# Norm copies ahead of squares, blocks split early, two products behind the batches

## The reference

```
# block 1
x = x + diff_attention(rms_norm(x, g), w_qkv, ...)       # 1024 -> 3072 columns, 8 double heads
x = x + conv_ffn(rms_norm(x, g), ...)                    # 1024 -> 5632 -> 1024
x = x + mla_attention(rms_norm(x, g), ...)               # rank 384 queries, rank 256 keys and values
x = x + conv_ffn(rms_norm(x, g), ...)
x = rms_norm(x, final_norm_g)
# block 2
b, c, h = split(rms_norm(x, g) @ w_in, 3)                # short convolution mixer
x = x + (b * conv3(c * h)) @ w_out
x = x + peer(rms_norm(x, g), ...)                        # 16384 experts, 8 heads x top 16
x = x + windowed_gqa(rms_norm(x, g), ...)
x = x + peer(rms_norm(x, g), ...)
out = rms_norm(x, final_norm_g_2)
```

## Time and profile before

| | |
|---|---|
| runs | 2628.58, 2632.16, 2633.97 us (median 2632.16) |
| profiled execution | 2633.33 us, span 2631.4 us |
| TensorE busy | 2527.1 us, 96% |
| VectorE busy | 1971.2 us, 75% |
| ScalarE busy | 1288.7 us, 49% |
| GpSimd busy | 749.9 us, 28% |
| mean granted TensorE clock | 0.987 |
| DMA | 424.66 MB, mean 161 GB/s |

### The profile page before, as it was taken

One profiled execution on the slowest core, in us unless ns is written; L12 is line 12 of the kernel. 1 busy time (PEld: TensorE's weight loads), 2 busy tenths in 40 slices (PEclk: granted clock), 3 DMA queues, 4 the chain that ended last, 5 costly groups with the idle time before them and its releaser, 6 DMA issues.

```text
span 2631.4 us, 44294 instructions
## 1 busy us (share of the span) xinstructions
PE 2527.1 (96%) x14328; PEld 2219.6 (84%) x14328; DVE 1971.2 (75%) x3589; ACT 1288.7 (49%) x1917; POOL 749.9 (28%) x754
## 2 busy tenths in 40 slices
PE   7889997999999999999999999899999999999998
PEld 6779976898889898888888888779898888888887
DVE  6868767787567998567777777688998577777776
ACT  4756556665544165544444444573165444444443
POOL 0400004000000101255555555230101255555554
PEclk9989999999999999999999999999999999999999
DMA  5145641556554523666666665434424666666664
GB/s 194 59 130 182 199 144 48 153 183 200 169 167 149 154 67 112 208 185 190 190 191 191 190 191 185 144 98 159 137 65 136 208 186 190 191 190 191 191 190 145
DMA packets 169937, 424.66 MB, mean 161 GB/s; under 512 B 13374, under 2 KB 65982, under 8 KB 169071
## 3 DMA queue, kind: packets, MB, share of 16 engines
q1 hardware_dynamic: 166832, 418.86, 51.5%
q10 hardware_dynamic: 3006, 4.49, 0.5%
HBM read 420.11 MB, written 3.18 MB: 161 GB/s over the span
## 4 chain that ended last, share of the span: by engine, by line
PE 88%; DVE 6%; ACT 3%; issue 2%; POOL 1%; DMA 0%; DVEq 0%; SPq 0%; POOLq 0%; ACTq 0%
PE PS L467 18%; PE PS L468 18%; PE PS L469 18%; PE PS L731 13%; PE PS L820 8%; PE PS L733 7%; PE PS L846 4%; DVE lo L1524 1%; PE PS L788 1%; ACT arena L1087 1%; PE PS L640 0%; DVE arena L1943 0%; DVE arena L1732 0%; DVE xx L1572 0%; ACT arena L1028 0%
## 5 line engine op out<-in xcount | busy, mean ns | idle before, releaser
L1524 DVE TENSOR_TENSOR lo<-raw,hi 128x1024 fp32r<-128x1024 f32 x716 | 1060.1, 1506 | 494.4 <-ACT hi L988 493.3
L988 ACT ACTIVATE hi<-raw 128x1024 fp32r<-128x1024 f32 x716 | 747.6, 1053 | 306.3 <-PE PS L469 287.9
L467 PE MATMUL PS<-hi,Ah 128*128 128x512 f32 x1024 | 402.6, 393 | 11.5 <-issue 5.4
L468 PE MATMUL PS<-lo,Ah 128*128 128x512 f32 x1024 | 402.1, 393 | 0.0
L469 PE MATMUL PS<-hi,Al 128*128 128x512 f32 x1024 | 399.6, 390 | 0.0
L731 PE MATMUL PS<-xx,hi 128*128 128x512 f32 x1504 | 371.4, 389 | 0.0
L731 PEld LDWEIGHTS PS<-xx,hi 128*128 128x128 f32 x1504 | 282.3, 188 | 58.6
L467 PE MATMUL PS<-xx,hi 128*128 128x256 f32 x1152 | 329.2, 286 | 1.4 <-DVE xx L1572 1.4
L468 PE MATMUL PS<-xx,hi 128*128 128x256 f32 x1152 | 328.2, 285 | 0.0
L469 PE MATMUL PS<-xx,lo 128*128 128x256 f32 x1152 | 327.9, 285 | 0.0
L1429 ACT ACTIVATE gl<-gl 128x256 f32<-128x256 f32 x188 | 78.6, 418 | 483.6 <-DVE gl L2276 483.6
(11 more groups left out here) (247 smaller groups left out, 3577.9 us busy)
## 6 DMA issues: line engine op xcount, KB each, us to landing
raw<-in_peer_u SPq DMA_DIRECT2D x256, 512.0 KB, 3.6
raw<-in_peer_v SPq DMA_DIRECT2D x256, 512.0 KB, 4.4
raw<-in_ffn_w_up SPq DMA_DIRECT2D x88, 512.0 KB, 3.6
raw<-in_ffn_w_down SPq DMA_DIRECT2D x44, 512.0 KB, 4.2
raw<-in_peer_w_q SPq DMA_DIRECT2D x32, 512.0 KB, 4.5
raw<-in_da_w_qkv SPq DMA_DIRECT2D x24, 512.0 KB, 4.4
raw<-in_conv_w_in SPq DMA_DIRECT2D x24, 512.0 KB, 3.8
raw<-in_attn_w_qkv SPq DMA_DIRECT2D x12, 512.0 KB, 4.3
```

Source lines behind the costliest of these rows:

```text
L467: pe.matmul(o, ah, bh, start=start, stop=False)
L468: pe.matmul(o, ah, bl, start=False, stop=False)
L988: cp.activation(hi[:, s, 0:size], raw[:, s, 0:size], ACT.Copy).then_inc(hi_made, 1)
L1524: V.tensor_tensor(lo[:, s, 0:size], raw[:, s, 0:size], hi[:, s, 0:size].bitcast(F32), ALU.subtract).then_inc(lo_made, 1)
```

## The change

It does four things. At the start, the gains of the first norm are loaded by themselves, the high and low copies come ahead of the squares with block 0 and 1 split among them, the other parameters are loaded by SP behind the first four blocks, and the parameter arithmetic moves to behind `lo` 7. `mla_ukv`'s blocks are split two behind group 1 of `mla_uq` and all four ahead of its loop. `cout`'s first four blocks are split beside the last group of `cin`, and TensorE does half `h` = 0 of them first, waiting only for the first half of `actL`. The leads are spread wider, and the last two stand behind batch 63; ScalarE does their GELUs behind the splits of `v` blocks 0 and 1.

```diff
@@ -100,7 +100,7 @@
 LEAD_FIRST = 20
-LEAD_AFTER = (-1, 3, 8, 13, 18, 23, 28, 33, 38, 43, 48, 53, 58, 63)
+LEAD_AFTER = (-1, 3, 8, 14, 19, 24, 30, 35, 40, 46, 51, 57, 63, 63)
 KEPT = LEAD - 2
@@ -260,8 +260,8 @@
-        lamv = view(1024, 4, DA_DH)
-        lamp = view(1024 + 256, 2, DA_DH)
+        lamv = view(29700, 4, DA_DH)
+        lamp = view(29700 + 256, 2, DA_DH)
         hotv = view(29000, 512)
@@ -532,23 +532,24 @@
-                early = RING if name in ("down0", "down1") else 0
+                early = RING if name in ("down0", "down1", "cout") else 0
+                first = 0 if name == "cout" else 1
                 if not early:
                     acc_ready(G0)
-                acc_ready(G0 + 1)
+                acc_ready(G0 + first)
                 for kc in range(early):
...
                     for t in range(TT):
-                        part(kc, t, 1)
+                        part(kc, t, first)
                 if early:
-                    acc_ready(G0)
+                    acc_ready(G0 + 1 - first)
                 for kc in range(kcs - 2):
...
                     for t in range(TT):
-                        for h in range(1 if kc < early else 2):
+                        for h in (1 - first,) if kc < early else (0, 1):
                             i = part(kc, t, h)
@@ -950,8 +951,8 @@
                 acc_free[G0 + g] = [(S("mix_read"), g + 1)]
-            pe.wait_ge(S("mix_lo"), 2)
-            wide("cout", actH, actL, KD)
+            pe.wait_ge(S("mix_lo"), 1)
+            wide("cout", actH, actL, KD, {4: lambda: pe.wait_ge(S("mix_lo"), 2)})
             for layer in range(2):
@@ -1164,19 +1165,32 @@
-            def load(dst, src):
-                act.dma_start(dst, src).then_inc(params_in, 16)
-            load(con[:, P:], consts[:, P:])
-            load(lamv, laid_rows[:, 0:4 * DA_DH].rearrange("o (k d) -> o k d", d=DA_DH).to_broadcast([P, 4, DA_DH]))
...
-            act.wait_ge(S("columns_in"), 16)
-            norm("n0", G_ATTN)
+            def first_squares(t):
+                for q in (2 * t, 2 * t + 1):
+                    w = quarters[q][1]
+                    cp.activation(XS[:, t, w], X[:, t, w], ACT.Square, scale=D ** -0.5,
+                                  accum_out=ss[:, q:q + 1]).then_inc(sq_made, 1)
+            def first_root(t):
+                act.wait_ge(ms_made, t + 1)
+                cp.activation(ss[:, 6 + t:7 + t], ss[:, 4 + t:5 + t], ACT.Sqrt).then_inc(rt_made, 1)
+            act.wait_ge(S("set_up"), 1)
+            cp.activation(small[:, 58:59], ss[:, 4:5], ACT.Sqrt)
+            act.wait_ge(S("first_gain_in"), 16)
+            turned("n0", G_ATTN, 0, range(4))
             splits_to(1)
+            turned("n0", G_ATTN, 0, range(4, KD))
+            splits_to(2)
+            act.wait_ge(S("x_in0"), 16)
+            first_squares(0)
+            splits_to(3)
+            act.wait_ge(S("x_in1"), 16)
+            first_squares(1)
+            first_root(0)
+            first_root(1)
             act.wait_ge(S("rstd_made"), 1)
@@ -1198,6 +1212,7 @@
                     qkv_copy(g, it)
+            act.wait_ge(S("columns_in"), 16)
             act.wait_ge(S("rel_table"), 1)
@@ -1324,13 +1339,11 @@
                         lambda t, g: arena[:, 1344 + t * 1536 + g * 512:1344 + t * 1536 + (g + 1) * 512],
-                        {0: lambda: turned("mck", G_MKV, MLA_QR // P)})
+                        {0: lambda: turned("mck", G_MKV, MLA_QR // P), 1: lambda: splits_to(plan["mla_ukv"][0] + 2)})
             B, G0 = plan["mla_ukv"]
-            splits_to(B + 1)
+            splits_to(B + 4)
             for g in range(4):
-                if g < 3:
-                    splits_to(B + g + 2)
                 act.wait_ge(split_used, B + g + 1)
@@ -1354,6 +1367,8 @@
                 else:
+                    if g == 5:
+                        splits_to(plan["cout"][0] + RING)
                     act.wait_ge(S("mix_y"), g - 3)
@@ -1411,12 +1426,12 @@
                         batch(b)
-                    for n, at_b in enumerate(LEAD_AFTER[:-1]):
+                    for n, at_b in enumerate(LEAD_AFTER[:-2]):
                         if at_b == b:
                             lead(LEAD_FIRST + n)
-                return lambda: lead(LEAD - 1)
-            def peer(layer, last_lead):
+                return lead
+            def peer(layer, lead):
                 B, _ = plan[f"peer{layer}"]
@@ -1441,8 +1456,8 @@
                     split(M + p)
-                    if p == 0:
-                        last_lead()
+                    if p < 2:
+                        lead(LEAD - 2 + p)
                 with act.Fori(0, (LEAD - 2) // 4, 1) as it:
@@ -1843,12 +1858,15 @@
             V.memset(ss, 1.0).then_inc(S("set_up"), 1)
+            dve.wait_ge(S("first_gain_in"), 16)
+            turned("n0", G_ATTN, 0, range(4))
+            splits_to(1)
+            turned("n0", G_ATTN, 0, range(4, KD))
+            splits_to(2)
             mean("n0", 0)
+            splits_to(3)
+            mean("n0", 1)
             root("n0", 0)
-            dve.wait_ge(S("columns_in"), 16)
-            turned("n0", G_ATTN)
-            mean("n0", 1)
-            splits_to(1)
             root("n0", 1)
@@ -1865,17 +1883,19 @@
-            splits_to(3)
-            dve.wait_ge(params_in, 16 * N_PARAMS)
-            link(V.tensor_tensor(lamp, lamv[:, 0:2, :], lamv[:, 2:4, :], ALU.mult))
...
+            def parameters():
+                dve.wait_ge(S("columns_in"), 16)
+                dve.wait_ge(params_in, 16 * N_PARAMS)
+                link(V.tensor_tensor(lamp, lamv[:, 0:2, :], lamv[:, 2:4, :], ALU.mult))
...
             splits_to(4)
@@ -1906,6 +1926,8 @@
                     V.tensor_copy(small[:, 5:6], neg_lam).then_inc(S("da_rows_ready"), 1)
+                if g == 0:
+                    parameters()
                 qkv_copy(g)
@@ -2110,11 +2130,15 @@
                 if g >= 4:
+                    if g == 5:
+                        splits_to(plan["cout"][0] + RING - 1)
                     dve.wait_ge(split_used, B + 4 * g + 4)
...
                     V.tensor_copy(rstd[:, 6:7], rstd[:, 0:1]).then_inc(S("mix_read"), 1)
+                    if g == 5:
+                        splits_to(plan["cout"][0] + RING)
                     dve.wait_ge(S("mix_hi"), g - 3)
@@ -2417,7 +2441,21 @@
                     sp.dma_start(con[:, 0:P], consts[:, 0:P]).then_inc(S("ident_in"), 16)
-            sp.dma_start(pT[:, :], laid_columns).then_inc(S("columns_in"), 16)
+            sp.dma_start(pT[:, 0:KD], laid_columns[:, 0:KD]).then_inc(S("first_gain_in"), 16)
+            def load(dst, src):
+                sp.dma_start(dst, src).then_inc(params_in, 16)
+            def parameters():
+                sp.dma_start(pT[:, KD:], laid_columns[:, KD:]).then_inc(S("columns_in"), 16)
+                load(con[:, P:], consts[:, P:])
+                load(lamv, laid_rows[:, 0:4 * DA_DH].rearrange("o (k d) -> o k d", d=DA_DH).to_broadcast([P, 4, DA_DH]))
...
@@ -2470,6 +2508,8 @@
                     for b in range(4):
+                        if B + 4 * g + b == RING:
+                            parameters()
                         block_in(B + 4 * g + b, w[:, 2 * b:2 * b + 2, c:c + 512])
```

More of the change, by code:

```diff
@@ L1866, in qkv_copy @@
                                     ALU.mult).then_inc(S("copied_dve"), 1)
-            splits_to(3)
-            dve.wait_ge(params_in, 16 * N_PARAMS)
-            link(V.tensor_tensor(lamp, lamv[:, 0:2, :], lamv[:, 2:4, :], ALU.mult))
-            link(V.tensor_reduce(lam_sum, lamp, AX.X, ALU.add))
-            exp_small(lam_sum, lamt[:, 0:2], lamt[:, 2:4].bitcast(mybir.dt.int32), lamt[:, 4:6], lamt[:, 6:8])
-            link(V.tensor_scalar(sinks, sinks, 0.25, None, ALU.mult))
-            link(V.tensor_scalar(neg_sinks, sinks, -1.0, None, ALU.mult))
-            link(V.tensor_scalar(subg, subg, 1.0 - LAMBDA_INIT, None, ALU.mult))
-            link(V.tensor_tensor(neg_lam, lam_sum[:, 1:2], lam_sum[:, 0:1], ALU.subtract))
-            link(V.tensor_scalar(neg_lam, neg_lam, -LAMBDA_INIT, None, ALU.add))
+            def parameters():
+                dve.wait_ge(S("columns_in"), 16)
+                dve.wait_ge(params_in, 16 * N_PARAMS)
+                link(V.tensor_tensor(lamp, lamv[:, 0:2, :], lamv[:, 2:4, :], ALU.mult))
+                link(V.tensor_reduce(lam_sum, lamp, AX.X, ALU.add))
+                exp_small(lam_sum, lamt[:, 0:2], lamt[:, 2:4].bitcast(mybir.dt.int32), lamt[:, 4:6], lamt[:, 6:8])
+                link(V.tensor_scalar(sinks, sinks, 0.25, None, ALU.mult))
+                link(V.tensor_scalar(neg_sinks, sinks, -1.0, None, ALU.mult))
+                link(V.tensor_scalar(subg, subg, 1.0 - LAMBDA_INIT, None, ALU.mult))
+                link(V.tensor_tensor(neg_lam, lam_sum[:, 1:2], lam_sum[:, 0:1], ALU.subtract))
+                link(V.tensor_scalar(neg_lam, neg_lam, -LAMBDA_INIT, None, ALU.add))
             splits_to(4)
@@ L2419, in _ @@
```

(8 more changed lines are left out.)

## The result

| | before | after |
|---|---|---|
| median of the runs, us | 2633.06 (2628.58 to 2633.99) | 2603.43 (2602.0 to 2604.29) |
| ratio | | 0.9889, interval 0.9877 to 0.9901 |
| profiled execution, us | 2633.33 | 2603.15 |
| span, us | 2631.4 | 2601.4 |
| mean granted clock | 0.987 | 0.992 |

The account below looks back on a forecast made before the run. TensorE was taken to bound the kernel (88% of the chain), gaining only where it waits or runs at 1.2 GHz. 9.2 + 8.0 + 7.1 - 3.9 = 20.4 us off the profiled 2633.3 gave 2612.9, forecast 2612, range 2603 to 2620.

Parts of the forecast that it names:

- Start, 9.2: At `da_qkv`: first product at 10.9 instead of 18.83, block 4 at 24.8 instead of 34.04, so 9.2 us earlier.
- Keys and values, 8.0: At `mla_ukv`: early splits remove TensorE's `lo` waits and slow clock; rows ready at 409.9 instead of 417.88, 8.0 us earlier.
- `cout`, 7.1: Convolution output: no wait left after `cin`, 7.1 us earlier, being 4.88 of idle and 2.2 of clock.
- Leads, -3.9: Behind batch 63: `Al` 2 comes late, TensorE goes on 0.46 later plus 1.5 of clock; both layers, 3.9 us lost.
- I take the 3.28 that the same work beside it cost: Behind the last leads: `Al` 2 takes 3.28 us as before, so TensorE goes on at 1041.1 after 3.7 idle.
- GpSimd gets in at once: At the value products: `Al` 2 ends by 1038.9, no clock fall, 3.3 us gained, total 2604.5; chance 0.15.
- GpSimd waits until VectorE pauses: At the value products: `Al` 2 ends only at 42.3, after VectorE's run; 7.9 us lost, total 2616; chance 0.28.

Follow-up runs that it names:

- only_start: The kernel before with the change at the start alone (gains first, arithmetic behind `lo` 7): 2622.95 us, ratio 0.9971.
- only_kv: The kernel before with `mla_ukv`'s early splits alone: 2625.24 us, ratio 0.9973.
- only_cout: The kernel before with `cout`'s early splits alone, leads in the old order: 2625.01 us, ratio 0.9977.
- after_swap: The changed kernel with ScalarE's high copy of lead 2 ahead of the split of value block 3 instead of behind it: 2604.67 us, ratio 0.9893.
- three small kernels: Kernels computing nothing of the reference, timing GpSimd's `Al` beside idle or busy VectorE, each run once: 0.72 us alone, at most 1.79, 1.79 and 1.61 beside VectorE.

## Why the prediction was right, and where it was wrong

- *Start, 9.2.* Right: 8.6 in the trace of after, 9.1 in that of only_start, 8.5 and 9.3 by the medians. The half of X landed 0.9 later than taken; TensorE's slow stretch was 5.7 us for 5.5 taken. The arithmetic (28.75 to 33.93) was hidden, with `lo` 8 at 34.96 where 35.3 was forecast. The edits at the start were only tried together, so how the 8.6 divide among the loads, the order of the copies and the arithmetic is not shown.
- *Keys and values, 8.0.* Right at the place (7.97), 7.0 by the median. In after 1.7 us were given back behind it, which the step did not have; in the trace of only_kv nothing was (9.8 less 1.9 in the table, 7.9). In after the clock is 0.84 in the mean over 398.7 to 420.0, in attention, where TensorE waits for other engines; the fall of before (401.0 to 403.9) had come ahead of it.
- *`cout`, 7.1.* Right: 7.1 in the trace, 7.2 by the median. The early half kept the clock at 1.00, so both terms, the idle and the clock, came.
- *Leads, -3.9.* Wrong in sign. The step that failed is "I take the 3.28 that the same work beside it cost": `Al` 2 took 1.25. The state beside it was not the same: VectorE's row, unbroken for 10.5 us before, now had a pause 0.9 us ahead of the request. That the pause is the reason is argued from the fourteen places, not shown by an edit. With 1.25 the idle is 1.3 and not 3.7, and the 1.5 of clock per layer doesn't come. Measured +1.35 per layer in the trace, 5.3 to 5.8 by the medians. The 3.28 had been seen at one place and twice over (both layers), which looked like a repeat and was one situation. The 188 `Al` of the main loop at 1.59 and the first pair, 1.59 together, were the other witnesses; they too were asked for at most 1.3 us behind a pause of VectorE or right behind GpSimd's last copy, and the new place is like them.
- *The rivals.* "GpSimd gets in at once", at 0.15 the third of the chances, is nearest to what happened in the leads: it priced them at 3.3 us gained, and 2.8 were measured at the two places. "GpSimd waits until VectorE pauses" (0.28) did not happen in after, though the rows of before, of only_cout and of after_swap show that GpSimd can be held like that. For the Trainium skill's rule ("SBUF — State Buffer", section "Who interferes with whom"): that the two exclude each other for a whole instruction agrees with 1.25 and 0.95 here and with all three small kernels (at most 1.79 beside a `lo` of 1.21); that a side is shut out for several instructions, as at the old place, is not what the rule says, and the prediction read it so.
- *The clock beside the steps.* 5.2 us of the 30.0 between the two spans are in no step: 2.7 before 240, 0.6 and 3.1 behind 1061, less 1.2 at the end. The first belongs to the profiled execution of before, not to the change: kernels with an untouched start show nearly as much. Part of the second may belong to the leads, whose medians (5.3 to 5.8) are above their 2.8.

Summed again with what was measured at the places: 8.6 + 6.3 + 7.1 + 2.8 = 24.8 against 20.4 forecast, of which 6.7 are the leads, less 0.6 and 1.7 for the first two. Taken from the profiled execution as the forecast was (2633.3 - 24.8 - 1.2), that gives 2607.3. So the time of 2603.43, inside the range by 0.4 and close to the 2604.5 of "at once", owes 4 us to the clock in places that no step names; that nearness is luck.

## What to carry to other kernels

Splits that wait behind the last use of another stage are worth their idle time plus a clock fall, and an early split gets both back; four such edits at four places simply add. A duration seen once per layer is one observation, however often it repeats: where one row says 3.28 and 188 rows of the same operation say 1.59, look at what the other engine had been doing before each, and ask which of them the new place will resemble. A small kernel that is to settle it must bring back that state, and not only the same pair of instructions. And a gain of under 2 us at one place should be read at that place, since the clock's falls elsewhere move a run by as much.

## What the runs showed of the hardware that was not expected

- Until 17.55 in after the matmuls start 0.43 us apart (12.85, 13.28), the pace of 1.2 GHz, and then 0.24 (17.55, 17.79), while the granted clock of that stretch reads 1.00 (table by stretch, first row). Before, it is the same (0.43 apart at 19.42 and 19.85). There the spacing of the matmuls tells the clock, not that column.
- A GpSimd low copy, 0.72 us alone, took 3.28 to 4.80 beside VectorE in the kernels with the old order, at every such place, and never over 1.81 in 158 trials of the small kernels or at the same place in the new order. At the fourteen places where VectorE had worked for 9.3 us or more without a pause and GpSimd had been idle for 6.8 us or more, it ended 0.6 us after VectorE's next pause began.
- VectorE pays for GpSimd's turn as well: a product of 0.41 us takes 0.95, a `lo` of 1.21 takes 1.76 right behind it.
